# Router logits computed transposed in two column halves, then turned back

## The reference

```python
x = x + g1 * (jnp.concatenate([attn, rec], axis=-1) @ lp['w_out'])
h2 = modulate(rms_norm(x, lp['norm2']), sh2, sc2)
# in moe(h2, ...):
p_grp = jax.nn.softmax(x32 @ wg + bg, axis=-1)          # 4 groups
g_sel = jnp.argmax(p_grp, axis=-1)
fine = (x32 @ we + be).reshape(-1, N_GROUPS, EXPERTS_PER_GROUP)   # 32 experts
fine_sel = jnp.take_along_axis(fine, g_sel[:, None, None], axis=1)[:, 0]
top_v, top_i = lax.top_k(fine_sel, TOP_K)               # 2 of 8
...
act = jax.nn.silu(hg) * hu * combine[:, :, None]
y = jnp.einsum('nef,efd->nd', act, w_down)
```

## Time and profile before

| what | us |
|---|---|
| median of 3 runs | 610.94 (610.49 to 611.8) |
| the profiled execution | 611.43 |
| its span, first to last instruction | 609.6 |
| one tile of the projection with its routing (PE, start to start of the logits) | 16.53 |
| one steady step of the experts (PE, gate-up start to start) | 12.2 |

### The profile page before, as it was taken

One profiled execution on the slowest core, in us unless ns is written; L12 is line 12 of the kernel. 1 busy time (PEld: TensorE's weight loads), 2 busy tenths in 40 slices (PEclk: granted clock), 3 DMA queues, 4 the chain that ended last, 5 costly groups with the idle time before them and its releaser, 6 DMA issues.

```text
span 609.6 us, 9282 instructions
## 1 busy us (share of the span) xinstructions
PE 581.9 (95%) x3274; PEld 325.0 (53%) x3275; DVE 346.5 (57%) x787; ACT 180.5 (30%) x377; POOL 109.0 (18%) x130
## 2 busy tenths in 40 slices
PE   5989999999998899999999999999999999997996
PEld 2544455455565667644555555555555555555452
DVE  2745898764464987754776787432433243322256
ACT  4203787711144877741101111111111111111110
POOL 4000011121242100000000001322232222221242
PEclk9999999999999999999999999999999999998999
DMA  8999833540018917809311999999999999999997
GB/s 323 379 368 360 325 132 145 206 153 1 1 37 236 341 44 227 357 24 395 151 53 47 373 380 394 405 419 417 420 417 392 414 417 422 420 418 417 418 386 306
DMA packets 48498, 175.89 MB, mean 289 GB/s; under 512 B 11633, under 2 KB 17789, under 8 KB 35408
## 3 DMA queue, kind: packets, MB, share of 16 engines
q1 hardware_dynamic: 36816, 155.06, 64.8%
q0 software_dynamic: 6688, 15.42, 7.2%
q10 hardware_dynamic: 4960, 4.96, 2.4%
HBM read 163.11 MB, written 21.14 MB: 302 GB/s over the span
## 4 chain that ended last, share of the span: by engine, by line
PE 76%; DMA 15%; SPq 3%; DVE 3%; issue 2%; ACTq 1%; ACT 0%; DVEq 0%; POOLq 0%
PE ps L1912 17%; PE ps L1690 11%; PE ps L1935 9%; PE ps L1615 9%; PE ps L1603 7%; PE ps L1730 4%; PE ps L1757 4%; DMA gate_w<-lru_wx 3%; DMA y_rows<-w,slot_row_now 3%; DMA w<-h_rows,slot_token 3%; PE ps L1739 3%; PE ps L1872 3%; DMA w_mod_ring<-w_mod 2%; PE ps L1578 2%; SPq L380 2%; PE ps L1524 2%
## 5 line engine op out<-in xcount | busy, mean ns | idle before, releaser
L1912 PE MATMUL ps<-expert_w,hT_mixT 128*64 128x256 f32 x1120 | 135.6, 391 | 4.3 <-issue 4.2
L1912 PEld LDWEIGHTS ps<-expert_w,hT_mixT 128*64 128x64 f32 x1120 | 85.2, 136 | 57.6 <-issue 14.1
L1603 PE MATMUL ps<-hT_mixT,w 128*128 128x128 f32 (+1 forms) x256 | 72.6, 437 | 1.2 <-DVE hT_mixT L999 1.2
L1690 PE MATMUL ps<-w,hT_mixT 128*128 128x512 f32 x160 | 71.9, 597 | 0.0
L1935 PE MATMUL ps<-expert_w,hT_mixT 128*64 128x512 f32 x276 | 66.0, 599 | 0.4 <-ACT hT_mixT L803 0.4
L798 ACT ACTIVATE hT_mixT<-ps 128x128 f32<-128x128 f32 x36 | 10.0, 278 | 177.8 <-PE ps L1912 177.8
L1603 PEld LDWEIGHTS ps<-hT_mixT,w 128*128 128x128 f32 x256 | 38.9, 191 | 35.8 <-issue 32.6
L1435 DVE SCALAR_TENSOR_TENSOR w<-ps,hT_mixT,w 128x1024 f32<-128x1024 f32 x17 | 21.8, 1284 | 57.8 <-PE ps L1935 50.3
L1615 PE MATMUL ps<-w_qkv,hT_mixT 128*128 128x512 f32 (+1 forms) x160 | 53.1, 488 | 0.0
L1388 DVE SCALAR_TENSOR_TENSOR hT_mixT<-hT_mixT,ps 128x128 f32<-128x128 f32 x36 | 10.4, 288 | 66.6 <-ACT hT_mixT L798 66.6
L1690 PEld LDWEIGHTS ps<-w,hT_mixT 128*128 128x128 f32 x160 | 29.1, 191 | 29.9 <-issue 29.7
(11 more groups left out here) (311 smaller groups left out, 757.4 us busy)
## 6 DMA issues: line engine op xcount, KB each, us to landing
expert_w<-exp_w_down SPq DMA_DIRECT2D x30, 1024.0 KB, 17.7
expert_w<-exp_w_gate SPq DMA_DIRECT2D x27, 1024.0 KB
expert_w<-exp_w_up SPq DMA_DIRECT2D x27, 1024.0 KB
w_mod_ring<-w_mod SPq DMA_DIRECT2D x14, 1024.0 KB, 6.5
y_rows<-zero_rows POOLq DMA_DIRECT2D x10, 512.0 KB, 6.1
expert_w<-y_rows SPq DMA_DIRECT2D x10, 512.0 KB, 8.9
recurrence<-w_mod SPq DMA_DIRECT2D x8, 512.0 KB, 9.6
w<-w_in SPq DMA_DIRECT2D x4, 1024.0 KB, 16.8
```

The lines of the kernel that those rows point to most:

```text
L1603: ins = pe.matmul(ps[:, bank, 0:n], w1v[:, c, m * P:(m + 1) * P], HM[:, c, lo:lo + n], start=(c == 0), stop=(c == DC - 1))
L1690: ins = pe.matmul(ps[:, 2 * (t % 2) + half, :], HM[:, c, t * P:(t + 1) * P], w1v[:, c, half * 512:(half + 1) * 512], start=(c == 0), stop= ...
L1912: ins = pe.matmul(ps[r, 2 + k, 0:2 * P].rearrange("p (k f) -> p k f", k=2), xT[:, c, r], gate_up(i)[:, :, c, k:FF:FC], start=(c == 0), sto ...
```

## The change

The two operands of the logits product trade places. Now 36 columns of the router matrix are the weights, and the 128 tokens of the transposed tile stream through; the even chunks go to columns 0 to 35 of the array, the odd ones to columns 64 to 99, so two products stand side by side. The result is the transposed logits in two halves (`lgT`, bank 5 of PSUM, rows 0 to 35 and 64 to 99). A new ACT copy (`lgT_out`, L763 of the changed kernel) brings it to SBUF, and one more product with `fold`, two stacked identities, adds the halves and turns them back to 128 x 36. Rows 36 to 63 of that bank are cleared once, with a memset on DVE in `biases`; `fold` is built by one DVE add.

Where things stand in the order: the transposed product keeps the old place, but all of `x1T`'s ACT pieces are waited for at its start and DVE's at its seventh chunk (before, from the fifth chunk and the seventh). One chunk of the projection follows it, then the turning product, then three chunks (before: four chunks between the logits' end and the same place). In the last tile a `keep_clock` of 256 columns stands between the two. On ACT the copy stands ahead of the squares of the next half tile, and in the last tile ahead of the DMA of `numbers` (L779). On POOL two semaphores become one that counts both.

```diff
+        fold = par[:, 5 * DC:5 * DC + NG + NE]
...
+        def lgT_of(t):
+
+            return HM[0:SLOTS + NG + NE, 7, P:2 * P] if t == NT - 1 else ring[0:SLOTS + NG + NE, HOME[4], D:D + P]
...
+            def lgT_out(t):
+
+                act.wait_ge(S["lgT"], 2 * t + 1)
+                act.activation(lgT_of(t), ps[0:SLOTS + NG + NE, 5, 2 * P:3 * P], ACT.Copy).then_inc(S["lgT"], 1)
+
...
                 x1_out(t, 1)
+                lgT_out(t)
                 squares_2(t + 1, 0)
...
             x1_out(NT - 1, 1)
+            lgT_out(NT - 1)
...
-                pool.tensor_copy(idxc[:, :], tid[:, bass.ds(n + 2, 1)]).then_inc(S["idxc_ok"], 1)
-                pool.wait_ge(S["idxc_ok"], n)
+                pool.tensor_copy(idxc[:, :], tid[:, bass.ds(n + 2, 1)]).then_inc(S["index_ok"], 1)
+                pool.wait_ge(S["index_ok"], n * 2 - 1)
...
+            dve.tensor_tensor(fold, ident[:, 0:NG + NE], ident[:, SLOTS:SLOTS + NG + NE], ALU.add)
...
+                dve.memset(ps[32:SLOTS, 5, 2 * P:3 * P], 0.0).then_inc(S["prepared"], 1)
...
+            def logits_turned(t):
+                pe.wait_ge(S["x1T_a"], 2 * t + 2)
+                for c in range(DC):
+                    if c == 6:
+                        pe.wait_ge(S["x1T_v"], t + 1)
+                    at = c % 2 * SLOTS
+                    ins = pe.matmul(ps[at:at + NG + NE, 5, 2 * P:3 * P], rwm[:, t // LT, c, :], x1T_of(t)[:, c, :],
+                                    start=(c < 2), stop=(c >= DC - 2))
+                ins.then_inc(S["lgT"], 1)
+
             def logits(t):
                 if t == 0:
-                    pe.wait_ge(S["prepared"], 4)
                     pe.wait_ge(S["st_ev"], 1)
                 else:
                     pe.wait_ge(S["lg_ev"], t)
                     pe.wait_ge(S["rank_rd"], t)
-                pe.wait_ge(S["x1T_a"], 2 * t + 1)
-                for c in range(DC):
-                    if c == 4:
-                        pe.wait_ge(S["x1T_a"], 2 * t + 2)
-                    if c == 6:
-                        pe.wait_ge(S["x1T_v"], t + 1)
-                    ins = pe.matmul(ps[:, 7, 0:NG + NE], x1T_of(t)[:, c, :], rwm[:, t // LT, c, :], start=(c == 0), stop=(c == DC - 1))
-                ins.then_inc(S["lg_mm"], 1)
+                pe.wait_ge(S["lgT"], 2 * t + 2)
+                pe.matmul(ps[:, 7, 0:NG + NE], lgT_of(t), fold[0:SLOTS + NG + NE, :], start=True, stop=True).then_inc(S["lg_mm"], 1)
...
                 project(t, 0, range(4, DC))
+                logits_turned(t - 1)
+                project(t, 1, range(0, 1))
                 logits(t - 1)
-                project(t, 1, range(0, 4))
+                project(t, 1, range(1, 4))
...
             keep_clock(1)
             x1_turn(NT - 1, 1)
-            logits(NT - 1)
+            logits_turned(NT - 1)
             pe.wait_ge(S["gated"], 2 * NT - 2)
             pe.wait_ge(wgu_in[0], 64)
+            keep_clock(1, 256)
+            logits(NT - 1)
             keep_clock(4)
```

More of the change, by code:

```diff
@@ L249, in build @@
             "qsq qss qrs qnorm kc_ok rot qT qT_a qT_v ckT s_mm nbias prob prob_n pT pT_a "
-            "o_mm mixT out_mm gated x1 ssq2 rs2 h2 x1T_mm x1T_a x1T_v lg_mm lg_ev "
+            "o_mm mixT out_mm gated x1 ssq2 rs2 h2 x1T_mm x1T_a x1T_v lgT lg_mm lg_ev "
             "mod2_in bc_ok shift_in g2_in route_in prepared bias_mm "
             "pair_ok rank_mm rank_rd slot slot_mm tid_ok gexp_in gexp route_ok "
-            "out_done v p act xg_in xt_mm gu_mm dn_mm xT_v xT_a th_ok act_ok aT_mm aT_ok y_v idxc_ok pidc_ok y_out "
+            "out_done v p act xg_in xt_mm gu_mm dn_mm xT_v xT_a th_ok act_ok aT_mm aT_ok y_v index_ok y_out "
             "y_zero gu_half base stepw late_mm late_ok now gsel chosen tail_mm fin sg_ok turn cache_out st_col st_t st_ev").split()}
@@ L897, in step_of @@
                 pool.wait_ge(S["y_out"], 16 * (n + 1))
-                pool.tensor_copy(pidc[:, :], pid[:, bass.ds(n, 1)]).then_inc(S["pidc_ok"], 1)
-                pool.wait_ge(S["pidc_ok"], n)
+                pool.tensor_copy(pidc[:, :], pid[:, bass.ds(n, 1)]).then_inc(S["index_ok"], 1)
+                pool.wait_ge(S["index_ok"], n * 2)
                 pool.wait_ge(S["y_v"], n + 2)
@@ L1773, in x1_turn @@
                 else:
-                    pe.wait_ge(S["prepared"], 5)
+                    pe.wait_ge(S["prepared"], 6)
                 for c in range(4 * half, 4 * half + 4):
@@ L1821, in _, with keep_clock @@
                 project(t, 1, range(5, DC))
-            def keep_clock(count):
+            def keep_clock(count, n=512):
                 for _ in range(count):
-                    pe.matmul(ps[:, 3, :], ident[:, :], ring[:, HOME[0], 0:512], start=True, stop=True)
+                    pe.matmul(ps[:, 3, 0:n], ident[:, :], ring[:, HOME[0], 0:n], start=True, stop=True)
             def slot_tokens(out, tiles, steps):
```

## The result

The changed kernel takes 615.06 us (median of 7 runs, 613.89 to 618.45) against 610.94 for the kernel before in the same session (7 runs). The ratio is 1.0054 [1.0032, 1.0076]: some 3.3 us slower, between 2.0 and 4.6. The forecast was slower by 1.8, 612.7. The measured median lies above its own range of 612.0 to 613.6 and 0.5 above the wide one of 610.6 to 614.6. So direction and place came out and the size did not: the forecast is 1.5 short of 3.3, and between 0.2 and 2.8 short over the interval.

A forecast was written before the change was run, and what follows sets the result against it. PE and DVE order bounds until 361, then the weight stream. x1 of the last half tile 1.10 later plus 0.70 in the last tile gave 1.80, so 612.7 us; own range 612.0 to 613.6, wide range 610.6 to 614.6.

The forecast's parts named there:

- The product itself: Logits product on PE: transposed 1.26 plus turning product 0.22, 1.48 us instead of 1.78, saving 0.30 per tile.
- The wait that takes its place: Tiles 0 to 2: choice 0.56 us later, PE waits 0.61 at the rank product, each tile 0.30 longer, 0.90 in all.
- if nobody waits: Condition on PE's saving of 0.30 us in each tile from the transposed and turning products.
- The last tile: Last tile's logits, covered by nothing: transposed product, copy and turning product make the choice 0.70 us later.
- The term of 1.10: Tile 3: choice 1.46 us later, less DVE's 0.36 idle, puts x1 of the last half tile 1.10 later.
- the whole 1.80 is passed on: Routing to expert stage: DMA engines run dry before h2's issue, so the 1.80 us delay reaches the end in full.
- Rival 1: Weight stream hides most of the delay in PE's 3.95 us wait; 0.6 to 1.2 slower, about 611.8; chance 0.15.
- Rival 2: Logits product under 0.96 us, no switching cost: not slower, 611.3 to 611.4; chance 0.16, including up to 0.07 for faster.
- Rival 3: Logits passes with 36 columns don't run side by side: 5.7 us slower, 616.6; chance 0.07.
- Rival 4: PE's clock falls in its new pauses of some 0.6 us; if in the last tile, 616.7; chance 0.06.

The follow-up runs named there:

- Experiment 4: Changed kernel with stated register bounds and the rank product of tiles 0 to 3 one projection chunk later; 612.76 us, before 611.9, ratio 1.0014.
- experiment 3: Changed kernel with stated register bounds and the last tile's logits as before the change; 612.88 us, before 611.9, ratio 1.002.
- experiment 5: Kernel before, with stated register bounds and two 512-column filler products on PE ahead of the last tile's logits; 614.76 us, before 611.9, ratio 1.0049.
- experiment 6: Changed kernel with stated register bounds, rank product one chunk later and last tile's logits as before; 610.72 us, before 611.68, ratio 0.9984.
- experiment 7: Kernel of experiment 6 with POOL's memset of the gather's tile also waiting for tile 3's choice; 611.06 us, before 611.68, ratio 0.9988.
- experiment 2: Changed kernel with stated register bounds and all eight transposed products in one column half, one after another; 618.71 us, before 611.9, ratio 1.0109.
- experiment 1: Changed kernel again, only stating bounds for most numbers loaded into registers in the expert stage; 614.6 us, before 611.5, ratio 1.0049.

## Why the prediction was right, and where its size was off

**The product itself: right, in its sum more than in its parts.** 16 passes took 1.00 where 1.11 was estimated from the attention's pairs. The chunk behind them took 0.96 to the start of the turning product (290.91 to 291.87) instead of 1.02. So from the first transposed pass to the choice it is 2.31 instead of 2.47. But that first pass starts 0.14 later than the first pass of before (289.91 for 289.77), 0.05 of it from ahead of the routing; for the other 0.09 the prediction had no term. That the choice came within 0.02 of its forecast is in part luck, two errors that cancel. The Trainium skill, TensorEngine Tiling (Array Packing), Theoretical Speedup, gives up to 2x for a dimension of at most 64. The traces agree for the passes (1.87 in one half against 1.00 in two). The same page, PSUM Bottleneck, says that tiling doesn't speed up the way out of PSUM, and the traces agree: ACT's copy takes 0.28 and, with the second product, stands on the path to the choice.

**The wait that takes its place: right.** The choice 0.54 later against 0.56, PE idle 0.44 to 0.47 instead of 0.61, and 0.25 lost per tile instead of 0.30. Experiment 4 shows by removing it that this wait turned PE's gain into a loss: without it a tile gains 0.37, where the forecast had 0.30 "if nobody waits".

**The last tile: right,** 0.68 against 0.70; experiment 3 takes it away alone.

**The term of 1.10 was mis-sized.** "That instruction is 1.46 - 0.36 = 1.10 later" measured 1.44. The shift itself was 1.28 instead of 1.46; but the step costed the choice of tile 3 as a block that is as long wherever it stands. It slid by 1.28 under POOL's memset, whose start hangs on PE's transposes and moved 0.43 only, and one of its instructions took 0.48 longer. So two errors stand in the term, -0.18 and +0.48, and 0.04 has no account. Both instructions were in the timeline of before, 0.59 apart (344.66 and 345.25); I looked at what waits for the choice, and not at what runs beside it.

**The term "the whole 1.80 is passed on": the result is right, its reason not borne out.** With 2.12 in place of 1.80 the profile has 2.12 at the first step of the experts and at h2's issue, and PE's wait unchanged; and in experiment 5 a pure delay comes out in full or with more. The reason given was that the DMA engines run dry at 356 and wait for h2. In the changed kernel they don't run dry there: in the window 358 to 360, around h2's issue, their share is 1.03 (at 269 GB/s), and at 366 the stream is behind by 0.8 us only, the 0.82 of its first issue (1.16 was forecast). It loses the next 1.6 us between 366 and 376, with the engines busy. There the weights that refill the places of the first step are asked for 2.12 later (SP at 367.81 for 365.69), as these issues wait for PE's products, and the first gather is in flight. Which of the two holds the stream up, no run separates.

**What stays open.** In the profiled execution 0.69 was added between the first step and the second, by the longer first gather. In the seven profiles whose chain runs over this gather it takes 8.90 to 10.79; in experiments 6 and 7 PE goes on 8.6 after its issue. The order is not that of its start: it takes 10.47 in experiment 4, where it is issued 0.3 after that of the kernel before, and 9.58 in the changed one, 2.1 after. But in all five profiles where it is issued 2 or more later it is longer than in the kernel before, 9.10 to 10.79. Whether it is longer for a reason in the change, or scatters and fell that way, one profile of each kernel can't tell. It may be the part of the loss above 2.1, if there is one: the interval begins at 2.0. So 2.1 of the loss is accounted for, and the other 1.2 of the 3.3 is open. No run took the gather's delay by itself.

**The rivals.** Rival 1 fell with experiment 5 and the 3.87 of the wait. Its stream was indeed 0.8 behind at 366, but made nothing up. Rival 2 needed a product under 0.96 with no cost for the switch; it took 1.00, and the choice came 0.54 later, not 0.26. Rival 3 fell with the 1.00, and experiment 2 gave its price. Rival 4: the clock granted in the last tile stayed at full speed through the waits of 0.32 and 0.47, the window of which is

```profile
352.00:354.00 2.00, 1.53 (x21) 1.09 (x19) 1.48 (x4) 0.85 (x3) 1.45 (x2) 1.00 0.90 270
```

with 1.00, the 2.4 GHz level, in the third column from the end, where the earlier trace rows had 0.50.

## What to carry to other kernels

A faster product is worth what the step that waits for its result gains, not what its engine saves: count to the next consumer, with every copy and second product that the new layout needs, and move the place where the other engine's result is wanted along with it. Where the saving only pays under cover, use the new form only where there is cover; here tiles 0 to 3 in halves with the rank product moved, and the last tile as it was, turned +0.5% into -0.2% [-0.32, +0.01], a loss into no change or a small gain. And when a chain of small instructions slides, look at what it slides under on the other engines.

## What the runs showed that was not expected

- A 32-column fp32 TENSOR_SCALAR of DVE in SBUF that starts beside POOL's 0.95 us memset doesn't end before it: 0.72 instead of 0.24, in six kernels alike (the changed one and experiments 1 to 4 and 6); in the kernel before, the TENSOR_TENSORs beside the same memset, from 345.38 on, kept their 0.17 to 0.18. Starting the memset later removed it. The Trainium skill, SBUF, SBUF: two separate sides, describes the port pair that DVE and GpSimd share as an exclusive lock that whoever starts first holds for its whole instruction, for DVE's operations in a 2-port mode but not for two-input ones beside a GpSimd operation that reads nothing. The trace agrees for the two-input ones. For the TENSOR_SCALAR it fits: the trace doesn't name the mode it ran in, and it ended 0.04 behind the memset, not another 0.24.
- A pause of PE of 3.9 near the end of a stream of weights is no slack. In kernels with a routing from 0.92 shorter to 6.4 longer it stayed at some 3.1 to 4.0 in all, in some split in two, while the end moved with the routing.
- The same indirect gather of one tile took between 8.6 and 10.79 from issue to landing while the DMA engines were full. From 366 to 376 the busy share was 1.05 in the kernel before and 0.99 in the changed one, 6% less, and the rate 387 and 319 GB/s, 18% less: the share alone doesn't tell how much is moved.
- The granted clock of PE fell to 0.50 behind a pause of 1.65 in one profile (experiment 5, 382 to 384) and stayed at 1.00 behind pauses of 1.82 and 2.14 at the same place in two others (experiments 4 and 2).
